# Hand-off order in a chunked RWKV-7 recurrence: inverse levels kept as I + X, copies moved from VectorE to ScalarE

## What is computed

```python
def step(S, inp):
    r_t, w_t, k_t, v_t, a_t, b_t = inp
    sa = jnp.einsum('bhvk,bhk->bhv', S, a_t)
    S = S * w_t[:, :, None, :] + sa[..., :, None] * b_t[..., None, :] + v_t[..., :, None] * k_t[..., None, :]
    y = jnp.einsum('bhvk,bhk->bhv', S, r_t)
    return S, y
```

## Time and profile before

| | |
|---|---|
| median of 3 runs | 3405.2 us (3399.24 to 3406.45) |
| the profiled execution | 3386.05 us, span 3384.7 us |
| mean granted PE clock | 0.936 of 2.4 GHz |
| PE busy | 3063.1 us, 90%, 19574 instructions |
| DVE busy | 2033.0 us, 60%, 3132 instructions |
| ACT busy | 1105.0 us, 33%, 1685 instructions |
| POOL busy | 91.1 us, 3%, 101 instructions |
| DMA | 345.56 MB, 102 GB/s on average |

### The profile page before, as it was taken

The page is one execution under the profiler, slowest core; times in us unless marked ns, Lnnn a source line. Parts: engine busy times, 40 slices in busy tenths (PEclk is TensorE's granted clock), DMA queues, the critical chain, the costliest instruction groups (busy, mean ns, idle before and its releaser), DMA issues.

```text
span 3384.7 us, 45906 instructions
## 1 busy us (share of the span) xinstructions
PE 3063.1 (90%) x19574; PEld 2499.1 (74%) x19577; DVE 2033.0 (60%) x3132; ACT 1105.0 (33%) x1685; POOL 91.1 (3%) x101
## 2 busy tenths in 40 slices
PE   6998899998988998986988778799999998799999
PEld 5876787886766787873757777678887787678887
DVE  5856895876576885866436777644444254545353
ACT  2334332223263431322324333242123343442121
POOL 0000000000000000000001211000000001100000
PEclk8998999998998998997988888799999997999999
DMA  8751454544512444540310000222332220023232
GB/s 238 176 181 43 159 181 149 177 161 150 180 47 82 167 131 163 185 143 14 108 24 8 11 12 7 73 86 95 100 100 76 88 99 13 7 75 97 91 99 87
DMA packets 236401, 345.56 MB, mean 102 GB/s; under 512 B 19605, under 2 KB 121949, under 8 KB 236197
## 3 DMA queue, kind: packets, MB, share of 16 engines
q1 hardware_dynamic: 217780, 327.27, 30.1%
q10 hardware_dynamic: 18416, 15.36, 1.7%
HBM read 340.45 MB, written 2.15 MB: 101 GB/s over the span
## 4 chain that ended last, share of the span: by engine, by line
PE 69%; DVE 19%; ACT 5%; DMA 5%; issue 1%; SPq 0%; DVEq 0%; ACTq 0%
PE bank L141 67%; DVE w_tiles L150 3%; DVE w_low L150 3%; DVE ada_acc L162 2%; PE bank L144 2%; ACT w_high L147 1%; ACT stage L147 1%; DMA weight_ring<-in_f_w_down 1%; DMA first_ada<-in_w_ada 1%; DVE x_natural L150 1%; DVE u_low L150 1%; DMA weight_ring<-in_f_w_up 1%; DMA weight_ring<-in_d_w_in 1%; DVE x_natural L162 1%; DVE stage L150 1%
## 5 line engine op out<-in xcount | busy, mean ns | idle before, releaser
L150 DVE TENSOR_TENSOR w_low<-weight_ring,w_high 128x2048 fp32r<-128x2048 f32 (+2 forms) x212 | 463.9, 2189 | 609.2 <-ACT w_high L147 609.2
L147 ACT ACTIVATE w_high<-weight_ring 128x2048 fp32r<-128x2048 f32 (+2 forms) x212 | 388.1, 1831 | 767.6 <-DMA weight_ring<-in_mlp_down 171.3
L141 PE MATMUL bank<-u_high,w_high 128*128 128x512 f32 x1472 | 583.7, 397 | 14.4 <-DVE w_low L150 5.4
L141 PE MATMUL bank<-u_low,w_high 128*128 128x512 f32 x1472 | 576.7, 392 | 0.0
L141 PE MATMUL bank<-u_high,w_low 128*128 128x512 f32 x1472 | 576.5, 392 | 0.0
L141 PE MATMUL bank<-w_high,u_high 128*128 128x512 f32 x896 | 354.8, 396 | 11.4 <-DVE u_low L150 6.5
L141 PE MATMUL bank<-w_low,u_high 128*128 128x512 f32 x896 | 351.0, 392 | 0.0
L141 PE MATMUL bank<-w_high,u_low 128*128 128x512 f32 x896 | 350.9, 392 | 0.0
L141 PEld LDWEIGHTS bank<-u_high,w_high 128*128 128x128 f32 x1472 | 278.7, 189 | 84.6 <-DVE u_low L150 17.0
L141 PEld LDWEIGHTS bank<-u_high,w_low 128*128 128x128 f32 x1472 | 278.5, 189 | 59.4
L141 PEld LDWEIGHTS bank<-u_low,w_high 128*128 128x128 f32 x1472 | 278.8, 189 | 56.3
(11 more groups left out here) (388 smaller groups left out, 4337.4 us busy)
## 6 DMA issues: line engine op xcount, KB each, us to landing
ada_ring<-in_mod_w SPq DMA_DIRECT2D x48, 1024.0 KB, 7.4
weight_ring<-in_f_w_up SPq DMA_DIRECT2D x44, 1024.0 KB, 5.1
ada_ring<-in_w_ada SPq DMA_DIRECT2D x40, 1024.0 KB, 7.3
weight_ring<-in_mlp_up SPq DMA_DIRECT2D x32, 1024.0 KB, 5.4
weight_ring<-in_mlp_down SPq DMA_DIRECT2D x32, 1024.0 KB, 5.0
weight_ring<-in_f_w_down SPq DMA_DIRECT2D x24, 768.0 KB, 4.7
weight_ring<-in_m_w_in SPq DMA_DIRECT2D x16, 1024.0 KB, 9.9
weight_ring<-in_d_w_in SPq DMA_DIRECT2D x12, 1024.0 KB, 5.2
```

The source lines that it names most:

```text
L141: return self.e.matmul(out, l, r, start=start, stop=stop, skip_group_check=True)
L147: return self.e.activation(out, in_, f, **kw) if self.live else QUIET
L150: return self.e.tensor_tensor(out, a, b, op) if self.live else QUIET
```

## The change

1. **PE one step earlier.** The empty first step of `pe_w_vectors` goes. `window` with three stages now gives the inverse stage its first step, counted, and then the vectors stage its free one. On PE that puts lora directly behind G.
2. **Masks.** DVE makes G1 and W for both heads first; the two masks of G2 come in a step of their own behind.
3. **I + X.** DVE writes X as I + X from the bank (the constant `w.stack` holds the identity for each head). Then W (I + X) is the new T and (I + X) W the new W, complete in the banks, and both are copied out by ACT. DVE's additions to T and W go.
4. **KT** is copied out by ACT, behind BT, no longer by DVE.

```diff
     def pe_w_vectors(self, pe, w, p):
         o = w.sets[p % 2]
-        yield
         pe.wait_ge(self.wkv_wa_in, p)
...
-        self.free[2], self.free[3] = (self.A, "w BT", p), (self.V, "w KT", p)
+        self.free[2], self.free[3] = (self.A, "w BT", p), (self.A, "w KT", p)
...
     def act_w_vectors(self, a, w, p):
         a.activation(o["BT"], self.bank[2][:], ACT.Copy).then_inc(*self.A.up("w BT", p))
+        a.activation(o["KT"], self.bank[3][:], ACT.Copy).then_inc(*self.A.up("w KT", p))
...
     def dve_w_vectors(self, v, w, p):
-        v.wait_ge(self.T, "w bt", p)
-        v.tensor_copy(o["KT"], self.bank[3][:]).then_inc(*self.V.up("w KT", p))
...
     def pe_w_inverse(self, pe, w, p):
-                if l == 1:
-                    pe.wait_ge(self.A, "w t0", p, h)
-                else:
-                    pe.wait_ge(self.V, "w t", p, h, l - 1)
+                pe.wait_ge(self.A, "w t", p, h, l - 1)
...
-                pe.wait_ge(self.A, "w x", p, h, l)
-                pe.wait_ge(self.V, "w w", p, h, l - 1)
+                pe.wait_ge(self.V, "w x", p, h, l)
+                if l > 1:
+                    pe.wait_ge(self.A, "w w", p, h, l - 1)
...
     def act_w_inverse(self, a, w, p):
         for l in range(1, 6):
-            for h, hd in enumerate(w.heads):
-                a.wait_ge(self.T, "w x", p, h, l)
-                a.activation(hd["X"][:, 0:TT * CH], self.bank[6 + h][:, 0:TT * CH], ACT.Copy).then_inc(*self.A.up("w x", p, h, l))
-                yield
             yield
             yield
+            for h, hd in enumerate(w.heads):
+                if l < 5:
+                    a.wait_ge(self.T, "w tx", p, h, l)
+                    a.activation(hd["T"], chunks(self.bank[h][:, 0:TT * CH]), ACT.Copy).then_inc(*self.A.up("w t", p, h, l))
+                a.wait_ge(self.T, "w wx", p, h, l)
+                a.activation(hd["W"], chunks(self.bank[6 + h][:, 0:TT * CH]), ACT.Copy).then_inc(*self.A.up("w w", p, h, l))
+                yield
...
     def dve_w_inverse(self, v, w, p):
-            for g, b, key in (("G1", 4 + h, "w g1"), ("G2", 6 + h, "w g2")):
-                v.tensor_tensor(hd[g].rearrange("p t a s -> p t (a s)"), quarters(self.bank[b][:]), spread(w.both), ALU.mult).then_inc(
-                    *self.V.up(key, p, h))
+            v.tensor_tensor(hd["G1"].rearrange("p t a s -> p t (a s)"), quarters(self.bank[4 + h][:]), spread(w.both), ALU.mult).then_inc(
+                *self.V.up("w g1", p, h))
...
-            yield
+        yield
+        for h, hd in enumerate(w.heads):
+            v.tensor_tensor(hd["G2"].rearrange("p t a s -> p t (a s)"), quarters(self.bank[6 + h][:]), spread(w.both), ALU.mult).then_inc(
+                *self.V.up("w g2", p, h))
+        yield
         yield
         yield
         for l in range(1, 6):
+            for h, hd in enumerate(w.heads):
+                v.wait_ge(self.T, "w x", p, h, l)
+                v.tensor_tensor(chunks(hd["X"][:, 0:TT * CH]), chunks(self.bank[6 + h][:, 0:TT * CH]), spread(w.stack), ALU.add).then_inc(
+                    *self.V.up("w x", p, h, l))
+                yield
             yield
             yield
-            for h, hd in enumerate(w.heads):
-                if l < 5:
-                    v.wait_ge(self.T, "w tx", p, h, l)
-                    v.wait_ge(self.V)
-                    v.tensor_tensor(hd["T"], hd["T"], chunks(self.bank[h][:, 0:TT * CH]), ALU.add).then_inc(*self.V.up("w t", p, h, l))
-                v.wait_ge(self.T, "w wx", p, h, l)
-                v.wait_ge(self.V)
-                v.tensor_tensor(hd["W"], hd["W"], chunks(self.bank[6 + h][:, 0:TT * CH]), ALU.add).then_inc(*self.V.up("w w", p, h, l))
-                yield
...
 def window(*stages):
     runs = [[g, 0, n] for g, n in stages]
     if len(stages) == 3:
-        next(stages[-1][0])
+        next(stages[1][0])
+        runs[1][1] += 1
+        next(stages[2][0])
```

More of the change, by code:

```diff
@@ L2220, in pe_w_inverse @@
         blocks = [(t, hs(c), slice(t * CH, (t + 1) * CH)) for t in range(TT) for c in range(2)]
-        pe.wait_ge(self.A, "w BT", p)
-        pe.wait_ge(self.V, "w KT", p)
+        pe.wait_ge(self.A, "w KT", p)
         for h, hd in enumerate(w.heads):
@@ L2243, in pe_w_inverse @@
                 m = pe.matmul(self.bank[h][c, at], hd["W"][c, t, :], self.ident[c, c], True, True)
-            m.then_inc(*self.T.up("w t0", p, h))
-            self.free[h] = (self.A, "w t0", p, h)
+            m.then_inc(*self.T.up("w tx", p, h, 0))
+            self.free[h] = (self.A, "w t", p, h, 0)
             yield
@@ L2257, in pe_w_inverse @@
                 m.then_inc(*self.T.up("w x", p, h, l))
-                self.free[6 + h] = (self.A, "w x", p, h, l)
+                self.free[6 + h] = (self.V, "w x", p, h, l)
                 yield
@@ L2268, in pe_w_inverse @@
                     m.then_inc(*self.T.up("w tx", p, h, l))
-                    self.free[h] = (self.V, "w t", p, h, l)
+                    self.free[h] = (self.A, "w t", p, h, l)
                 for t, c, at in blocks:
@@ L2272, in pe_w_inverse @@
                 m.then_inc(*self.T.up("w wx", p, h, l))
-                self.free[6 + h] = (self.V, "w w", p, h, l)
+                self.free[6 + h] = (self.A, "w w", p, h, l)
                 yield
         for h, hd in enumerate(w.heads):
-            pe.wait_ge(self.V, "w w", p, h, 5)
+            pe.wait_ge(self.A, "w w", p, h, 5)
             pe.wait_ge(*self.free[h])
@@ L2327, in act_w_inverse @@
         for h, hd in enumerate(w.heads):
-            a.wait_ge(self.T, "w t0", p, h)
-            a.activation(hd["T"], chunks(self.bank[h][:, 0:TT * CH]), ACT.Copy).then_inc(*self.A.up("w t0", p, h))
+            a.wait_ge(self.T, "w tx", p, h, 0)
+            a.activation(hd["T"], chunks(self.bank[h][:, 0:TT * CH]), ACT.Copy).then_inc(*self.A.up("w t", p, h, 0))
             yield
         for l in range(1, 6):
-            for h, hd in enumerate(w.heads):
-                a.wait_ge(self.T, "w x", p, h, l)
-                a.activation(hd["X"][:, 0:TT * CH], self.bank[6 + h][:, 0:TT * CH], ACT.Copy).then_inc(*self.A.up("w x", p, h, l))
-                yield
             yield
             yield
+            for h, hd in enumerate(w.heads):
[5 more added lines that the diff above has]
+                yield
         for h, hd in enumerate(w.heads):
```

## The result

| | before | changed |
|---|---|---|
| median of 4 runs | 3402.22 us (3393.35 to 3406.45) | 3447.27 us (3440.63 to 3449.16) |
| ratio | | 1.0132, 95% interval 1.0106 to 1.0159 |
| the profiled execution | 3386.05 us | 3449.05 us |
| DVE / ACT busy | 2033.0 / 1105.0 us | 1999.1 / 1131.8 us |

What follows compares the result with a forecast made beforehand. PE was taken to hold the end for 69%, DVE 19%, with PE's order deciding. +6.05 us a window plus 1.6 for clock, six windows +45.9, other windows added: +48.1 on the median 3405.2, 3453 us; bounds 3427 to 3485.

Steps and rivals of the forecast that it cites:

- rival 2: Whole kernel: early waits let DVE and ACT work ahead, so delays are absorbed; about +2 us a window, 3417 us; chance 0.08.
- Head: From G to level 1: mask waits vanish, but cum waits 2 us for ACT's sigmoids; gives 0.1 us a window.
- Chunk: PE's chunk, now directly behind state product 3, waits for DVE's E4: +2.8 us a window.
- Level 3: Level 3 products wait for X, which stands on DVE behind norm and KM: +2.6 us a window.
- Bt: Bt, now ahead of PE's x5, waits 2.4 us for DVE where it waited 1.48: +0.9 us a window.
- W5: ACT issues the square ahead of the W5 copy, so PE waits 1.1 us ahead of r: +0.95 us a window.
- The clock term: Full windows: new idle gaps bring one more fall of PE's clock, +1.6 us a window; bounds 0 and 4.8.
- The first windows: First window with an inverse +2.8 us, from waits at cum, rt and bt; the very first, with gate products, +0.4.
- The table load: ACT's load ahead of the sigmoids takes 1.28 us; the skill's extra drain of about 1.38 us was left out.
- Rival 1: Whole kernel: DVE's load, not the order, decides; losing 4.6 us of DVE work a window gives 3377 us; chance 0.12.
- rival 3: Full windows: every new gap drops the clock, giving 3480 us or so; part of the forecast's own range, no separate chance.
- Rival 4: ACT's exponentials between W2 and T3 keep the copies on the path; time stays 3453 us either way; no chance given.

Runs made afterwards that it cites:

- step alone: The kernel before with only PE's vectors steps one slot earlier and the new `window`; sums, masks and KT as before: 3478.44 us, ratio 1.0235.

## Why the prediction was right, and where not

Forecast were 3453 us, 48.1 above the kernel before, with bounds of 3427 to 3485 (the lower one adds up to +23, not +22) and the range widened down to 3410 for rival 2; measured are 3447.27, 45 above. The mechanism is the one that was forecast: PE lost its slot behind DVE and ACT and waits for them. That the time came within 6 us is partly luck, since two errors point opposite ways: the six full windows took 36.1 us more in the profile for 45.9 forecast, and the two in front of them 24.7 for 3.2. And the profiles' difference of 63 us is not the medians' 45. By its steps:

- **Head.** Forecast were 2.0 us of waiting for the sigmoids; measured 0.57 ahead of cum and 1.50 ahead of the state product in front of it, together 2.07. Right in size, but three quarters of it for another reason: s0 stands on DVE behind the G2 masks (1.28 us) and the decay product (0.81). Cum ran at the low clock here, 3.65 us, and still ended 12.0 us after G began, ahead of the stated bounds of 13.1 to 14.7, since G and lora ran at the full clock. In this window the head gave 1.9 us instead of 0.1.
- **Chunk** +2.8, with 2.3 if E3 runs in 0.7: measured 2.25, and E3 took 0.69. **Level 3** +2.6: 2.83. **Rt** +1.7: 1.53. **Bt** 2.4: 2.56. **Ahead of gh** 1.4: 1.20. **W5** 1.1: 0.54, the one of these that was off by half.
- **Sum without the clock**: +6.05 us a window. PE's idle time in the six windows grew by 39.1 us, 6.5 each.
- **The clock term was mis-sized**, +1.6 a window. PE's busy time in the six windows, where the clock shows, is 3.0 us less than before in the one profile and 3.5 us more in the other that runs this order, so -0.5 to +0.6 a window. The new gaps did bring falls of the clock: in the walked window there are four short ones, each beginning within 1.2 us of the end of a wait (cum, chunk, bt, gh), though none behind the largest, 2.83 us at level 3. What the term missed is that the long low stretch behind G, which the prediction let stay, can go. Before, and then after up to the end of the first short fall:

```profile
1919.50:1933.20 13.70, 10.89 (x139) 9.77 (x133) 8.02 (x15) 4.48 (x8) 5.23 (x6) 0.50 0.01 2
```

```profile
1956.11:1964.60 8.49, 6.08 (x121) 5.38 (x122) 5.73 (x12) 2.85 (x5) 3.28 (x4) 1.00 0.04 9
1964.60:1968.00 3.40, 3.40 (x4) 0.90 (x4) 1.74 (x3) 0.29 (x1) 0.00 (x0) 0.50 0.02 5
```

- A gap of 2.86 us stands ahead of G in both. Before, the low clock followed within 1.3 us; here the head, with 0.34 us of idle up to the second state product, stayed at the full clock. The low stretches of the six windows add up to 96 us before and to 82 and 106 in the two profiles of the changed order, so which way the clock goes with the order is open.
- **The first windows were mis-sized.** Forecast +2.8 and +0.4; measured in the profile +9.1 and +15.6. What failed there is "eight gate products then bound the rest, and they end no sooner": it priced them at the clock of before. In the changed kernel rt and bt stop PE between the gate products (1.36 and 1.18 us), and the clock stayed low. Putting the first window's old order back took 15.8 us off that window, but only about 6 off the median.
- **The table load.** The sigmoids started 0.01 us after the table load of 1.28 us had ended (timeline of ACT: load at 1962.51, sigmoids at 1963.80), and cum waited 0.57. The drain that the Trainium skill (ScalarE: Activation LUTs, "What ACT_TABLE_LOAD costs") adds doesn't show; the sum was right to leave it out. The row that the prediction cites couldn't have told, since ACT stands idle for 2.23 us between load and sigmoids there, waiting for lora; another load of the kernel before (1.28 us from 1932.60) does, with the next operation at 1933.90.
- **Rival 1** (DVE's load decides, faster) fell: DVE's busy time in the six windows went from 231.75 to 204.99 us, and they grew. But it holds in a smaller sense that the prediction didn't have: with PE's early steps, I+X, masks and KT together are worth 1% (step alone 1.0235, whole change 1.0132), and nothing in PE's old order (1.0010). That it is I+X of the three is likely from DVE's work ahead of rt, but was not tried by itself in this order. **Rival 2** (absorbed) fell too, and so did **rival 3** (every gap drops the clock, 3480): behind the 2.83 us at level 3 of the walked window the clock stayed full, 1.00 from 1978.3 to 1995.3 us. **Rival 4**'s exponentials did not bind.
- **Attribution.** The prediction booked +2.6 at level 3 to I+X. The runs book 1.6 of it to chunk's place. And cum early, for which it saw a wait and no gain, is the one early step that pays when the later ones stay where they were.

## What to carry to other kernels

In queues interleaved by hand, count for every value that crosses engines how many slots its reader stands behind its writer. PE had one slot of slack on DVE and ACT; giving it up for lora's sake cost four waits a window, though nothing was added and the busiest helper had less to do. Move one step at a time: the early steps whose inputs are ready and which fill a wait (lora with cum) gain 0.5%, the other three lose 1.9% together. In these runs a helper's load mattered where its queue was late for a reader: taking the sums, the second masks and KT out of DVE's way was worth 1% in one order and nothing in the other.

## What was not expected of the hardware

The granted clock stayed at 0.50 in the gate window of the changed kernel for 48 us in all, 44.5 of them in one piece from 1742.8 to its end. The stretches of 1755 to 1768 us, with the wait ahead of rt and the start of that ahead of bt, and of 1768 to 1786, bt and then gate products alone (128x512, every second one with 32 rows):

```profile
1755.00:1768.00 13.00, 11.28 (x18) 3.65 (x17) 7.62 (x12) 5.05 (x9) 0.00 (x0) 0.50 0.00 1
1768.00:1786.00 18.00, 17.18 (x24) 5.60 (x24) 0.00 (x0) 4.05 (x8) 0.00 (x0) 0.50 0.06 15
```

In the second PE was busy for 17.18 of 18 us and the clock did not rise. The same window before, with the rise at 1752.3:

```profile
1735.20:1752.30 17.10, 6.74 (x8) 2.18 (x9) 0.00 (x0) 2.29 (x4) 0.00 (x0) 0.50 0.43 34
1752.30:1771.03 18.73, 17.75 (x54) 6.78 (x53) 12.00 (x20) 9.22 (x16) 0.00 (x0) 1.00 0.03 8
```

The rise came after 6.74 us of products without a gap, cum (128 rows) the last of them; from then on a gate product took half the time. The step alone showed the same as the changed kernel: 53.7 us for the window, 47 of them at the low clock. All other variants had 17 to 34 us of low clock there, and those with PE's old order in this window 17 in four profiles and 27 and 31 in two, so a part is chance. The 47 and 48 us of the two stand out of it. Bt early alone is not what sets them apart: the variant with all three engines one slot earlier has bt at the same place of PE's order, and had 24 us. What in that mix keeps the clock down was not tried.
